# Gated stages: gate and up blocks by a seven-product scheme over halves of channels and tokens, weight sums on VectorE

## The reference, cut to what matters

```python
D_MODEL, SEQ, D_FF = 1024, 512, 2816
def _rmsnorm(x, g):
    y = x32 * lax.rsqrt(jnp.mean(x32 * x32, axis=-1, keepdims=True) + RMS_EPS)
    return (y * g.astype(jnp.float32)).astype(x.dtype)
def _swiglu(x, w_gate, w_up, w_down):
    return (jax.nn.silu(x @ w_gate) * (x @ w_up)) @ w_down
x = x + 0.5 * _swiglu(_rmsnorm(x, ffn1_norm[l]), ffn1_w_gate[l], ffn1_w_up[l], ffn1_w_down[l])
```

## Time and profile before

| | us |
|---|---|
| time, median of 3 runs | 3194.55 (3194.05 to 3194.66) |
| span of the profiled execution | 3192.7 |
| what lies around the span (median less span) | 1.85 |
| PE busy in the span | 3141.7 (98%) |
| DVE busy | 1712.6 (54%) |
| ACT busy | 1157.7 (36%) |
| POOL busy | 530.2 (17%) |

### The profile page before, as it was taken

How to read it: one execution, slowest core, us unless ns; L and a number is a source line. 1 busy time by engine, 2 the same in 40 slices (tenths; PEclk the granted TensorE clock), 3 DMA queues, 4 the chain that set the end, 5 groups by cost and what they waited for, 6 DMA issues and landing times.

```text
span 3192.7 us, 42566 instructions
## 1 busy us (share of the span) xinstructions
PE 3141.7 (98%) x14928; PEld 2525.4 (79%) x14928; DVE 1712.6 (54%) x2735; ACT 1157.7 (36%) x1889; POOL 530.2 (17%) x483
## 2 busy tenths in 40 slices
PE   8999999999999999999999999999999999999998
PEld 6888876788888888776888878677888886778887
DVE  4434477543445434586543444557647546576474
ACT  4324246322223222344322332645324335443242
POOL 0000336200020000355100030231000432310003
PEclk9999999999999999999999999999999999999999
DMA  3345331233333333321333333122333231223332
GB/s 118 100 141 148 100 106 41 86 103 90 97 99 92 106 89 107 81 63 47 92 104 89 101 93 117 43 67 66 107 88 102 78 94 47 61 72 104 92 98 81
DMA packets 528422, 288.10 MB, mean 90 GB/s; under 512 B 13630, under 2 KB 520225, under 8 KB 528314
## 3 DMA queue, kind: packets, MB, share of 16 engines
q1 hardware_dynamic: 523706, 273.40, 29.6%
q0 software_dynamic: 4608, 13.30, 1.4%
HBM read 284.38 MB, written 10.02 MB: 92 GB/s over the span
## 4 chain that ended last, share of the span: by engine, by line
PE 85%; DVE 6%; issue 3%; ACT 3%; POOL 1%; SPq 1%; DMA 0%; DVEq 0%; ACTq 0%; POOLq 0%
PE bank L1964 66%; PE bank L1982 5%; PE bank L2201 3%; PE bank L2311 2%; PE bank L1999 2%; PE bank L2353 2%; PE bank L2376 1%; PE bank L2134 1%; PE bank L2040 1%; DVE w_lo L1339 1%; ACT w_hi L841 1%; DVE scaled_g L1452 0%; DVE tap_g L1541 0%; ACT tap_v L1004 0%; POOL probs_mix L734 0%
## 5 line engine op out<-in xcount | busy, mean ns | idle before, releaser
L841 ACT ACTIVATE w_hi<-w_raw 128x1024 fp32r<-128x1024 f32 (+1 forms) x471 | 527.7, 1120 | 1395.8 <-PE bank L1964 712.6
L1964 PE MATMUL bank<-h_hi,w_hi 128*128 128x512 f32 x2420 | 949.9, 393 | 11.2 <-DVE w_lo L1339 7.4
L1964 PE MATMUL bank<-h_hi,w_lo 128*128 128x512 f32 x2420 | 942.3, 389 | 0.0
L1964 PE MATMUL bank<-h_lo,w_hi 128*128 128x512 f32 x2408 | 937.8, 389 | 0.0
L1339 DVE TENSOR_TENSOR w_lo<-w_raw,w_hi 128x1024 fp32r<-128x1024 f32 (+1 forms) x439 | 608.2, 1386 | 523.8 <-ACT w_hi L841 523.8
L1964 PEld LDWEIGHTS bank<-h_hi,w_hi 128*128 128x128 f32 x2420 | 453.8, 188 | 119.9 <-issue 15.6
L1964 PEld LDWEIGHTS bank<-h_hi,w_lo 128*128 128x128 f32 x2420 | 453.9, 188 | 95.8
L1964 PEld LDWEIGHTS bank<-h_lo,w_hi 128*128 128x128 f32 x2408 | 451.7, 188 | 95.3 <-issue 1.7
L1964 PE MATMUL bank<-act_hi,w_hi 128*128 128x512 f32 x924 | 359.5, 389 | 0.0
L1964 PE MATMUL bank<-act_hi,w_lo 128*128 128x512 f32 x924 | 359.4, 389 | 0.0
L1964 PE MATMUL bank<-act_lo,w_hi 128*128 128x512 f32 x924 | 359.4, 389 | 0.0
(11 more groups left out here) (344 smaller groups left out, 4100.7 us busy)
## 6 DMA issues: line engine op xcount, KB each, us to landing
w_raw<-in_ffn_w_gate_dram SPq DMA_DIRECT2D x88, 512.0 KB, 3.8
w_raw<-in_ffn_w_up_dram SPq DMA_DIRECT2D x88, 512.0 KB, 3.8
w_raw<-in_ffn_w_down_dram SPq DMA_DIRECT2D x64, 704.0 KB, 4.5
w_raw<-in_ffn_w_in_dram SPq DMA_DIRECT2D x88, 512.0 KB, 3.8
w_raw<-in_ffn_w_out_dram SPq DMA_DIRECT2D x32, 704.0 KB, 4.5
w_raw<-in_w_in_dram SPq DMA_DIRECT2D x34, 512.0 KB, 3.8
w_raw<-in_a_w_qkv_dram SPq DMA_DIRECT2D x24, 512.0 KB, 3.7
w_raw<-in_w_out_dram SPq DMA_DIRECT2D x16, 512.0 KB, 3.8
```

Source lines behind the costliest of these rows:

```text
L841: nc.scalar.activation(split_home(c)[0][:, 0:nk, 0:cols], raw[c % 2][:, 0:nk, 0:cols], ACT.Copy).then_inc(hi_ready, 1)
L1964: mm = nc.tensor.matmul(result(c)[0:cols, :], w[:, k, 0:cols], x[k], start=(k == 0 and n == 0), stop=(k == nk - 1 and n == 2))
```

## The change

Of every gated stage the first two pairs stay as they were. The other 20 (9 in the first half, 11 in the second) go by seven products instead of eight. Let G1, G2 and U1, U2 be the gate and the up weights of channels 0 to 511 and 512 to 1023, and X11, X21, X12, X22 the input of those channels (first index) for tokens 0 to 255 and 256 to 511 (second index). Four sums of weights are made for each pair by DVE (`weight_sums`): U1+U2, U1+U2-G1, G1-U1, and G2-(U1+U2-G1). Four sums of inputs are made once for each stage by POOL (`token_sums`) from an unsplit copy of the input that ACT makes (`full_input`), and split like everything else (`token_high`, `token_low`).

A *product* is 4 blocks by 3 matmuls of 256 columns, 12 matmuls. In PE's order they are P1 (G1), P2 (G2), then P4 of the pair before (U2, the last of that pair), P6, P5, P7, P3. P1, P6, P7 and P4 add up in one bank; in between ACT copies what the bank holds to `gate_sum` (`part_of`, after P1, P6 and P5), and DVE adds the copies to the other products (`gate_first`, `gate_last`, `up_cross`).

The buffer `ws` has seven slots, one for each product, each with a high and a low part, single. The multiplication of silu's output by `rstd` moves from DVE to POOL (`gate_scale`). The pairs are written out; there is no loop over them any more. The copies of bias rows that POOL issued at the head of the program (24 DMAs) now stand in the second half of the first stage.

The diff, cut:

```diff
+            def token_sums(name):
...
+                pool.wait_ge(full_ready, KT * FAST[name] + KT)
+                nc.gpsimd.tensor_tensor(t_raw[:, 0, :, :], h_full[:, 0:KH, t2], h_full[:, 0:KH, t1], ALU.subtract).then_inc(t_made, 1)
...
+            def gate_scale(name, hf, j):
...
+                pool.wait_ge(silu_ready, FF[name] + FH * hf - CONV_FF[name] + 1 + j)
+                nc.gpsimd.tensor_tensor(gated[:, :], gated[:, :], rstd[:, :], ALU.mult).then_inc(gate_ready, 1)
...
+            def full_input(name):
...
+                for k in range(KT):
+                    nc.scalar.activation(h_full[:, k, :], xres[:, k, :], ACT.Copy,
+                                         scale=pre_gain(name, k)).then_inc(full_ready, 1)
```

ACT, the written-out pairs:

```diff
+                    for j in range(j0, FH):
+                        more = j + 1 < FH
+                        part_of(hf, j, "P1", gate_sum[j % 2][:, HALF[0]], SUM_D[j % 2])
+                        sums_high(hf, j, True)
+                        if j > j0:
+                            silu(hf, j - 1)
+                        if more:
+                            raw_high(hf, j + 1)
+                        last_high(hf, j)
+                        part_of(hf, j, "P6", gate_sum[j % 2][:, HALF[1]], SUM_D[j % 2])
+                        if j > j0:
+                            product_high(hf, j - 1)
...
+                        if not more:
+                            hi(down, freed=(prod_done, product_count(name, hf, j, "P6")))
+                        part_of(hf, j, "P5", gate_sum[(j + 1) % 2][:, HALF[1]], SUM_F)
+                        if more:
+                            sums_high(hf, j + 1, False)
```

DVE, what goes of the pair and the written-out pairs:

```diff
-                        divided(at, scaled_g[:, :], jj)
-                        if at not in FIRST:
-                            lo(at + 2, jj)
-                        dve.wait_ge(silu_ready, a0 - CONV_FF[name] + 1 + j)
-                        nc.vector.tensor_tensor(gate_r[:, :], gated[:, :], rstd[:, :], ALU.mult).then_inc(gate_ready, 1)
...
+                    for j in range(j0, FH):
+                        more = j + 1 < FH
+                        if j > j0:
+                            gate_last(hf, j - 1)
+                            weight_sums(name, hf, j, True)
+                            sums_low(name, hf, j, True)
...
+                        gate_first(hf, j)
...
+                        else:
+                            product(hf, j - 1)
+                        if more:
+                            raw_low(name, hf, j + 1)
+                            weight_sums(name, hf, j + 1, False)
+                        last_low(hf, j)
+                        if j > j0:
+                            act_low(a0 + j, j - 1)
...
+                        if more:
+                            sums_low(name, hf, j + 1, False)
+                        else:
+                            lo(down)
+                        up_cross(hf, j)
```

PE, the products of a pair (`up_last` is P4 of the pair before):

```diff
+                for j in range(FAST_FROM[hf], FH):
+                    n, d, first = of_pair(name, hf, j), SUM_D[j % 2], j == FAST_FROM[hf]
+                    pe.wait_ge(low_part, 3 * n + 1)
+                    if j >= 2:
+                        pe.wait_ge(bank_free[1], XT_USES + (c + 1) // 2 + j - 1)
+                    product(d, 0, b11, True).then_inc(prod_done, 1)
+                    if n:
+                        pe.wait_ge(first_sum, n)
+                    product(SUM_A, 1, b21, True).then_inc(prod_done, 1)
+                    if not first:
+                        up_last(j - 1)
+                    pe.wait_ge(part_copied, 3 * n + 1)
+                    pe.wait_ge(low_part, 3 * n + 2)
...
+                    product(d, 2, t2s, False).then_inc(prod_done, 1)
...
+                    product(SUM_F, 3, t1s, True).then_inc(prod_done, 1)
+                    pe.wait_ge(part_copied, 3 * n + 2)
+                    pe.wait_ge(low_part, 3 * n + 3)
...
+                    product(d, 4, t3s, False).then_inc(prod_done, 1)
+                    pe.wait_ge(part_copied, 3 * n + 3)
+                    product(SUM_F, 5, b22, False).then_inc(prod_done, 1)
```

More of the change, by code:

```diff
@@ new lines, in fast_ff @@
+            def fast_ff(name, gate, up, down):
+                c = BASE[name]
+                for u in range(2 if c == 0 else 0, 4):
+                    load(c + u, (gate, up)[u % 2][:, :, P * (u // 2):P * (u // 2 + 1)])
+                for j in range(FAST_FROM[0], FH):
+                    fast_gate(name, 0, j, gate)
+                    fast_up(name, 0, j, up)
+                for n in range(KT):
+                    load_down(name, 0, n, down)
+                    if n == KT - 3:
+                        fast_gate(name, 1, 0, gate)
+                        fast_up(name, 1, 0, up)
+                for j in range(1, FH):
+                    fast_gate(name, 1, j, gate)
+                    fast_up(name, 1, j, up)
+                for n in range(KT):
+                    load_down(name, 1, n, down)
@@ L697, in store_bias_rows, with copy_bias_row @@
                 pool.wait_ge(tab_one, 16 * 3)
[L698 to L702, removed]
+            stored_rows = [0]
+            def copy_bias_row():
+                if stored_rows[0] == 24:
+                    return
+                r, h = divmod(stored_rows[0], 8)
+                stored_rows[0] += 1
+                row = bass.AP(brow_one[r].ap().tensor, h * SPAN, [[0, P], [1, SPAN]])
+                pool.dma_start(brow_d[r].ap()[h], row).then_inc(tab_dram, 16)
@@ L961, in down_parts @@
                     hi(c + 3, j)
-                if halves:
+                if halves or last:
                     return
@@ L1230, in _ @@
                     joint_root()
-                if kind(name) == "ffn":
+                if name in FAST:
+                    for n in range(3):
+                        token_high(name, n)
                     gated_ff(name)
@@ new lines, in down_blocks @@
+            def down_blocks(c, blocks, count, freed=None):
+                if blocks[0] == 0:
+                    pe.wait_ge(lo_ready, c + 1)
+                    pe.wait_ge(bank_free[0], XT_USES + freed // 2 + 1)
+                for k in blocks:
+                    pe.wait_ge(act_ready, count + k + 1)
+                    for n, (w, x) in enumerate(((w_hi, A_HI), (w_hi, A_LO), (w_lo, A_HI))):
+                        mm = nc.tensor.matmul(bank[c % 2][:, :], w[c % 2][:, k, :], x[k],
+                                              start=(k == 0 and n == 0), stop=(k == FH - 1 and n == 2))
+                if blocks[-1] == FH - 1:
+                    mm.then_inc(mm_done, 1)
@@ L2454, in _ @@
                 h0 = KT * PRE[name]
-                if kind(name) in ("ffn", "conv"):
+                if name in FAST:
+                    first_units(name, c, h0)
+                    gemm(c + 2, H_HI, H_LO, h_ready, h0)
+                    gemm(c + 3, H_HI, H_LO, h_ready, h0)
+                    for hf in range(HALVES):
+                        down, a0 = c + 30 * hf + 2 * FH, FF[name] + FH * hf
+                        fast_pairs(name, hf)
+                        if hf == 0 and name == stages[0]:
+                            channel_rows()
+                        gemm(down + 1, A_HI, A_LO, act_ready, a0)
+                        gemm_pairs(down, KT, A_HI, A_LO, act_ready, a0, first=1)
+                elif kind(name) == "conv":
                     for hf in range(HALVES):
```

355 lines of the change are left out of this document (306 added, 49 removed).

## The result

| | us |
|---|---|
| time before, median (4 runs) | 3194.41 (3194.05 to 3194.66) |
| time after, median (4 runs) | 3307.47 (3306.74 to 3312.51) |
| ratio after to before | 1.0347, 95% interval 1.0312 to 1.0382 |
| predicted | 3279 (3222 to 3335) |

A forecast was written before the change was run, and what follows sets the result against it. The bound moves from PE to a ring through DVE, ACT and POOL, 11.65 us a pair. Halves +7.6 and +7.1 and start 6.1 make 20.8 a stage, 83.2 for four, plus 1.5: +85, 3279 us (3222 to 3335).

The forecast's parts named there:

- the ring: Steady pair: a round of dependent work through DVE, ACT and POOL takes 11.67 us, about 11.65, against PE's 10.08.
- that rounding: Steady pair: ACT's rounding of the first sums takes 1.08 us beside 1.2 us of other DVE work, so costs nothing.
- the lock: Steady pair: POOL's gate scaling waits for DVE's two-tensor operation on SBUF to end, then takes its 1.15 us.
- The rival price of 2.55: POOL's gate scaling: 2.55 us as POOL's own price for 512 columns, the kernel some 90 us slower still; no separate chance.
- ring of 13.0 us: Steady pair: length of the round through DVE, ACT and POOL if 2.55 us were POOL's own price; no separate chance.
- P7 wait for the low part of the second sums: Steady pair: most of PE's 1.6 us of waits fall ahead of P7, which needs that low part.
- DVE's wait for POOL: Steady pair: DVE idles about 1.2 us behind POOL's gate scaling.
- The clock falls: Rival, steady pairs: at the lower clock a pair's matmuls take 20 us, the kernel near 3900 us; 2%.
- 6 us of idle PE at each start: Start of each stage: PE stalls 6.1 us before the first P1, four times; bounds 0 and 9.
- a wait at each half's end: Last pair of a half: P3 waits for ACT's copy of P5 and ends at 12.9 us; the pair takes 14.35.
- a granted clock under 1: Sign that would show the forecast wrong, listed beside a spacing near 10.1 us and PE waiting for DMA.
- The first two intervals: Start of a half: intervals of 10.65 and 10.6 us, shorter than the steady 11.65, since the ring fills up only then.

The follow-up runs named there:

- e2: Kernel after the change, with DVE making the next pair's first two weight sums directly behind this pair's last two: 3219.58 us, spacing 10.62.
- e7: Kernel after the change, with seven DVE operations (four weight sums, three low parts) cut to 32 columns of each half in most fast pairs: 3166.61 us.
- e6: Kernel after the change, with useless 128-column matmuls on PE ahead of each stage's first P1 and each half's last P3: 3301.44 us.
- e10: Kernel after the change, with the low part of the second weight sums made a one-input copy instead of a difference: 3270.11 us, single run.
- e5: Kernel after the change, with ACT's rounding and DVE's low part of G moved earlier at stage starts and token low parts moved: 3303.11 us.
- e3: Kernel after the change, with the gate scaled on DVE instead of POOL and the next pair's first two weight sums made earlier: 3214.80 us.
- e11: The e3 kernel, with POOL waiting for the previous pair's silu before each two bias-row transfers in the first stage: 3198.63 us.

## Why the prediction was right, point by point

**The mechanism was right.** The bound moved from PE to the ring; e2 takes one wait out of the ring and the pair shortens by 1.26 us, e7 takes DVE's work out and the spacing is PE's 10.08.

**The ring's size.** Forecast 11.67, measured 11.88, term by term from the rows above: both product halves 0.67 (0.66), low part of G 1.14 (1.14), first weight sum 0.78 (0.72), second and low part of U2 1.22 (1.20), activation's low part 0.66 (0.60), first sums' low part 1.15 (1.14), cross sum 0.33 (0.33), `gate_last` 0.52 (0.45), scaling and third sum 1.21 (1.20), fourth 0.72 (0.72), ACT 1.09 (1.08), low part and POOL together 2.39 (2.43). The 0.21 are mostly three places where DVE waits for its own result or for ACT's rounding of the first sums, each 0.06 or 0.07 dearer than forecast; that rounding was to cost nothing. Over the 14 steady intervals of a stage and four stages, 0.23 over the rounded 11.65 are 13 us of the 28 that the forecast lacked (113 against 85).

**POOL.** Its record is 1.79, it ends 1.14 after DVE, as forecast from the earlier trace rows. The Trainium skill, page "SBUF — State Buffer", section "SBUF: two separate sides", has the lock that the prediction weighed; the records of 1.28, 1.79 and 2.07 us agree with it for two operands. The rival price of 2.55 is out with the 1.28. Its ring of 13.0 us was reckoned with POOL waiting for DVE as well; without that wait it comes to some 12.4.

**Who releases P7.** The prediction had P7 wait for the low part of the second sums. That was wrong: the low part was there at 143.99, and ACT's copy of P6 only at 144.99, behind the rounding of these sums, silu and the roundings of G and U2. It cost nothing, since this chain too starts with DVE's fourth sum at 140.96. DVE's wait for POOL is 0.83 and not 1.2, because the first gate sum stands in between.

**The clock.** "The clock falls" was priced for steady pairs alone, and there it stayed at 1.00. The forecast itself had 6 us of idle PE at each start and a wait at each half's end, and asked nothing of the clock there. It named a granted clock under 1 as a sign that it was wrong, and 0.53 to 0.71 was measured in the two windows above: this sign came, in places that the forecast had not priced. e6 prices it at 6.0 us.

**Starts and ends.** In ffn1_1 the first P1 comes 22.2 us after the statistics matmul, 17.2 before: 5.0, forecast 6.1 (4.4 us too much in four stages). The first two intervals of the stage are 11.86 and 11.39 from P1 to P1 (starts at 1045.42, 1057.28 and 1068.67), forecast 10.65 and 10.6: 2.0 a stage, 8 in all. The clock has no part in them, for e6 has 11.87 and 11.38 at 1.00. Two of DVE's token low parts, 1.22 us each, stand among them (at 1047.02 and 1056.84), which the forecast counted in neither interval; the second half of the stage, without them, has 8.63 and 10.44, 19.1 in sum where 19.25 was forecast. That they are the cause was not tested. The last pair of a half, with the clock up (e6) and without the three down blocks in it, takes 14.6, forecast 14.35: 0.25 x 8 = 2. Ring 13, clock 6, first intervals 8, last pairs 2, less 4.4: some 25 of the 28 us. The first stage's second half has 0.9 more, the bias rows beside its loads. Some 2 us stay open. That 113 came out within the range owes little to errors that cancel: of the larger terms only the start was priced too dear.

## What to carry to other kernels

Before trading work of the bounding engine for work of idle ones, walk once around the loop through every engine that works in order: each place where one waits for an answer to its own last instruction adds the whole round trip, whatever its busy share says. Such a wait is filled by moving independent work directly behind the request; here one moved call gave back 88 of 113 us. And an operation that paces a queue does a second job: take it away, and what it held back comes in a burst.

## What the runs showed of the hardware

- The same gap of PE, 2.66 to 2.68 us, stands at the end of every half. The clock stayed at 1.00 behind it at 161, 353 and 766 us and fell at the five others, which cost 6.0 us together, 1.2 each. Behind the gaps at the four starts, 3.6 us in the first stage and 5.2 to 5.3 in the others, it fell each time. Matmuls of 128 columns, without use, put into these twelve gaps kept it at 1.00 (e6).
- POOL and DVE exclude each other both ways for operations on two tensors in SBUF: POOL's 1.28 us became 2.07 (e2), and DVE's 1.22 us became 2.82 (e5).
- A DVE operation on 1024 columns from two tensors took 1.22 us, from one tensor and a constant 0.69 (e10).
- Beside 18 transfers of 320 KB that went out within 10 us, loads of 512 KB landed in 16.5 to 19.6 us instead of 3.8 (e3); with the transfers paced the wait was gone (e11).
- Left open: what tells the ends of halves at which the clock fell from the others. No run varied it alone.
